# The S5 mixer's block kernel: two buffers, the diagonal on TensorE, and a new order of DMA issues on ScalarE

## The chip, the cores and the metric

The kernel runs on one core of one Trainium2 chip. The metric is the device time of one execution in microseconds; of several runs the median is taken. All data are fp32 (products use fp32 or its split in a high and a low part).

## What is computed

The program is two transformer-like blocks one behind the other. The change lies in the first, in one of its two mixers, the S5 mixer, which works on 64 groups of 16 channels with 64 complex states each:

```python
bu_re = jnp.einsum('blgh,gph->blgp', u, bb_re)
bu_im = jnp.einsum('blgh,gph->blgp', u, bb_im)
_, _, s_re, s_im = lax.associative_scan(combine, (a_re, a_im, bu_re, bu_im), axis=1)
y = (jnp.einsum('blgp,ghp->blgh', s_re, c_re.astype(f32))
     - jnp.einsum('blgp,ghp->blgh', s_im, c_im.astype(f32))
     + u * d_skip.astype(f32))
y = jax.nn.gelu(y.reshape(bsz, length, D_S5), approximate=False)
v = y @ w_glu.astype(f32) + b_glu.astype(f32)
y = v[..., :D_S5] * jax.nn.sigmoid(v[..., D_S5:])
```

The term `u * d_skip` is a diagonal matrix of 16 x 16 for each group. It can be added to the first tap (lag 0) of the kernel with which a group's inputs are convolved, and that is what is done here.

## The kernel before

The eight groups of a block are worked together, so there are eight blocks, i = 0 to 7 (NT = 8). Time is cut in pieces of LB = 8 steps. What lies within a piece is a product with a small lower-triangular block matrix (tile mt, made of the eight lags of the kernel ka); what crosses pieces goes through the states, with a scan over 65 pieces.

For block i these steps follow each other:

- VectorE, `s5_tables`: products of powers into ba and cab (L1342 to L1351). It waits for the k product of block i-1 and, ahead of writing cab (L1347), for the y product of block i-2.
- TensorE, `s5_bat_pe` (L1424): ba turned. ScalarE, `s5_bat_act` (L1508): the copy bat.
- TensorE, `s5_k_pe` (L1433): the eight lags of the kernel into PSUM. ScalarE, `s5_kernel_act` (L1516): the copy ka, in one buffer, for which it waits until the moves of block i-1 have landed (L1514); behind it the two copies to dec (L1519).
- VectorE, `s5_diagonal` (L1363, L1367): dd is d_skip on a diagonal; it is added to lag 0 of ka.
- ScalarE's DMA queue, `s5_move` (L1526): eight DMAs put ka, shifted by a lag each, into mt.
- TensorE, `s5_w_pe` (L1444), VectorE, `s5_scan` (L1379 to L1394), TensorE, `s5_y_pe` (L1457 from the states, L1465 from mt).
- ScalarE: Gelu into yk (L1559); its DMA queue, `s5_y_out` (L1538): eight DMAs write yk to memory, in another order of elements; GpSimd's queue, `s5_y_back` (L1330), reads it back as yf; ScalarE, `s5_hi` (L1530), and VectorE, `s5_lo` (L1399), split it into hhi and hlo for the gated unit.

The order on each engine is written out by hand. On VectorE (`s5_dve`) an iteration i is scan(i), diagonal(i+1), tables(i+2), lo(i-2). On ScalarE (`s5_act`) it is move(i+1), in some iterations the rows of the modulation (L762), Gelu(i), bat(i+2), y out(i), kernel copy(i+2), hi(i-1), in some iterations the columns of the modulation (L772). On TensorE (`s5_pe`) it is y(i), w(i+1), bat(i+2), k(i+2), in iterations 1, 3, 4, 6 and 7 the turn of the modulation (L780), and between all of them the products with the modulation's weights (L752), whose tile wada holds eight units and is loaded by SyncE's queue. These products belong to the second block of the network; they fill the time in which TensorE would wait. The gated unit (L338) follows the last iteration.

An engine that issues a DMA executes the issue in its own program order.

## Time and profile before

| | us |
|---|---|
| median of 3 runs | 2908.52 |
| lowest, highest run | 2907.16, 2919.92 |
| span of the profiled execution | 2895.8 |
| TensorE busy in it | 2800.7 |
| VectorE busy | 1503.3 |
| ScalarE busy | 1083.2 |
| GpSimd busy | 1268.2 |

The span goes from the first to the last instruction of the one profiled execution. The eight blocks lie between about 355 and 500 us of it. In the rows below, PE is TensorE, PEld its weight loads, DVE VectorE, ACT ScalarE, POOL GpSimd, SP SyncE; a name with q behind it (ACTq) is that engine's DMA issues. Times are in us unless ns is said; a row of the timeline is start, duration, engine, line, operation, output<-inputs, count, and in brackets the idle time ahead of it and what ended it. "Issue" stands where the profile shows nothing that was waited for. Issues of DMAs are not counted as busy.

### The profile page before, as it was taken

What the parts mean: (1) busy time and instruction counts of PE and PEld (TensorE: products, weight loads), DVE (VectorE), ACT (ScalarE), POOL (GpSimd) and SP (SyncE); (2) the same over time, 40 slices, a digit from 0 to 9 for tenths busy, and PEclk for the clock granted to TensorE, in tenths of its full rate; (3) what the DMA queues carried; (4) which work ended last, traced back from release to release, by engine and by line L of the source; (5) the groups of instructions that cost most, each with busy time, mean ns of one, the idle gap of its engine ahead of it and who ended that gap; (6) DMA issues with size and microseconds to landing.
All of it is one profiled execution on the core that took longest, in us unless ns stands there. A gap on an engine that the chain in (4) does not pass through costs nothing.

```text
span 2895.8 us, 41246 instructions
## 1 busy us (share of the span) xinstructions
PE 2800.7 (97%) x15682; PEld 2290.9 (79%) x15682; DVE 1503.3 (52%) x1968; ACT 1083.2 (37%) x1662; POOL 1268.2 (44%) x696
## 2 busy tenths in 40 slices
PE   7999988999999999999999999999999999999998
PEld 6985744878888888877787888888887778788887
DVE  6865585353332345358875532422454887452535
ACT  4435223333332323235543422322343554342433
POOL 3444201434354264278842323222347884344343
PEclk9999999999999999999999999999999999999999
DMA  5335498323232243432222212121233222233232
GB/s 174 99 102 203 148 312 239 123 86 104 80 110 86 90 129 118 157 104 90 70 87 66 73 52 72 65 66 59 62 106 111 94 66 88 80 102 95 94 102 73
DMA packets 116008, 306.89 MB, mean 106 GB/s; under 512 B 36176, under 2 KB 44496, under 8 KB 115344
## 3 DMA queue, kind: packets, MB, share of 16 engines
q1 hardware_dynamic: 87584, 284.49, 30.6%
q10 hardware_dynamic: 27712, 18.50, 2.3%
q8 instruction: 101, 1.65, 0.2%
q0 software_dynamic: 560, 1.84, 0.2%
q14 instruction: 51, 0.42, 0.0%
HBM read 294.95 MB, written 7.45 MB: 104 GB/s over the span
## 4 chain that ended last, share of the span: by engine, by line
PE 85%; DVE 4%; DMA 2%; issue 2%; POOL 2%; ACT 2%; DVEq 1%; ACTq 1%; SPq 0%; POOLq 0%
PE ps L304 41%; PE ps L338 17%; PE ps L329 6%; PE ps L1955 3%; PE ps L1951 3%; PE ps L1956 3%; PE ps L1959 3%; POOL wlo L265 2%; PE ps L2368 2%; PE ps L2028 1%; PE ps L2009 1%; DMA mt<-ka 1%; PE ps L752 1%; DVE nacc L451 1%; PE ps L1997 1%
## 5 line engine op out<-in xcount | busy, mean ns | idle before, releaser
L265 POOL TENSOR_TENSOR wlo<-wraw,whi 128x1024 fp32r<-128x1024 f32 x373 | 919.8, 2476 | 1316.1 <-ACT whi L257 1313.7
L257 ACT ACTIVATE whi<-wraw 128x1024 fp32r<-128x1024 f32 x373 | 392.1, 1055 | 458.0 <-PE ps L304 170.4
L304 PE MATMUL ps<-xah,whi 128*128 128x512 f32 x992 | 388.2, 391 | 1.7 <-issue 1.7
L304 PE MATMUL ps<-xal,whi 128*128 128x512 f32 x992 | 387.8, 391 | 0.0
L304 PE MATMUL ps<-xah,wlo 128*128 128x512 f32 x992 | 280.2, 391 | 0.0
L2254 DVE SCALAR_TENSOR_TENSOR co<-ub,vec,co 128x512 f32<-128x512 f32 (+1 forms) x216 | 255.7, 1222 | 4.2
L304 PEld LDWEIGHTS ps<-xah,whi 128*128 128x128 f32 x992 | 186.1, 188 | 42.7 <-issue 2.7
L304 PEld LDWEIGHTS ps<-xah,wlo 128*128 128x128 f32 x992 | 186.2, 188 | 40.0
L304 PEld LDWEIGHTS ps<-xal,whi 128*128 128x128 f32 x992 | 186.2, 188 | 40.1
L2355 POOL TENSOR_TENSOR co<-co,ct 128x512 f32<-128x512 f32 (+1 forms) x144 | 164.7, 1144 | 21.7 <-issue 1.8
L304 PE MATMUL ps<-hhi,whi 128*128 128x512 f32 x408 | 159.4, 391 | 0.0
L304 PE MATMUL ps<-hlo,whi 128*128 128x512 f32 x408 | 158.9, 389 | 0.0
L1113 DVE SCALAR_TENSOR_TENSOR res<-ps,mod,res 128x512 f32<-128x512 f32 (+1 forms) x64 | 47.6, 748 | 201.6 <-PE ps L329 110.0
L2711 DVE SCALAR_TENSOR_TENSOR f<-ps,vec,f 128x511 f32<-128x511 f32 x88 | 50.1, 611 | 196.7 <-ACT f L2672 196.7
L1955 PE MATMUL ps<-xah,whi 128*128 128x512 f32 x352 | 143.6, 408 | 4.2 <-DVE ub L2266 2.6
L2353 POOL TENSOR_TENSOR ct<-ub,vec 128x512 f32<-128x512 f32 (+1 forms) x144 | 136.7, 950 | 22.5 <-issue 12.4
L1956 PE MATMUL ps<-xal,whi 128*128 128x512 f32 x352 | 137.7, 391 | 0.0
L2669 ACT ACTIVATE f<-ps,vec 128x512 f32<-128x512 f32 x44 | 34.3, 778 | 187.0 <-PE ps L329 179.3
L1111 DVE TENSOR_TENSOR res<-res,ps 128x512 f32<-128x512 f32 x48 | 33.0, 687 | 132.1 <-PE ps L304 70.2
L304 PE MATMUL ps<-hhi,wlo 128*128 128x512 f32 x408 | 100.9, 389 | 0.0
L329 PE MATMUL ps<-xchi,whi 128*128 128x256 f32 x352 | 99.6, 283 | 0.0
L329 PE MATMUL ps<-xchi,wlo 128*128 128x256 f32 x352 | 99.4, 282 | 0.0
(415 smaller groups left out, 5978.5 us busy)
## 6 DMA issues: line engine op xcount, KB each, us to landing
wraw<-stream SPq DMA_DIRECT2D x425, 512.0 KB, 3.5
wada<-w_ada SPq DMA_DIRECT2D x56, 512.0 KB, 7.0
wraw<-w_ada SPq DMA_DIRECT2D x40, 512.0 KB, 3.8
biasb<-attn_bias ACTq DMA_DIRECT2D x32, 256.0 KB, 3.4
xin<-x0T SPq DMA_DIRECT2D x4, 528.0 KB, 6.2
s_u<-uk ACTq DMA_DIRECT2D x8, 264.0 KB, 2.7
res<-x0T ACTq DMA_DIRECT2D x1, 2048.0 KB, 9.3
outT<-res SPq DMA_DIRECT2D x4, 512.0 KB, 2.6
```

Source lines behind the costliest of these rows:

```text
L257: act.activation(whi[:, s], wraw[:, s], ACT.Copy).then_inc(hi_done[s], 1)
L265: pool.tensor_tensor(wlo[:, s], wraw[:, s], whi[:, s].bitcast(F32), ALU.subtract).then_inc(lo_done[s], 1)
L304: last = pe.matmul(ps[:, bank, 0:b - a], w[:, s, kt], x[:, kt, c0 + a:c0 + b], start=start, stop=stop)
L329: return pe.matmul(ps[:, R + s, 0:CTX], w[:, s, kt], part[:, kt], start=start, stop=stop)
L338: last = pe.matmul(ps[:, bank, 0:b - a], w[:, s, kt], x[:, kt, c0 + a:c0 + b], start=start, stop=stop)
L1951: last = pe.matmul(o, wraw[:, s, kt], x1[:, kt, 0:p.T], start=kt == 0, stop=kt == NT - 1)
L1955: pe.matmul(o, whi[:, s, kt], xah[:, kt, 0:p.T], start=kt == 0, stop=False)
L1956: pe.matmul(o, whi[:, s, kt], xal[:, kt, 0:p.T], start=False, stop=False)
L1959: last = pe.matmul(o, wlo[:, s, kt], xah[:, kt, 0:p.T], start=False, stop=kt == NT - 1)
L2254: dve.scalar_tensor_tensor(o, ub[:, m, k:k + p.T], colr(f"dw{p.l}", 1, k * 4 + m), o, ALU.mult, ALU.add)
L2353: pool.tensor_tensor(ct[:, 0:T], ub[:, m, k:k + T], colr(f"dw{l}", 1, k * 4 + m).to_broadcast([P, T]), ALU.mult)
L2355: ins = pool.tensor_tensor(o, o, ct[:, 0:T], ALU.add)
```

## The change

The tiles ka and dd get two buffers, ka1 in a place where the last parts of hlo will be, dd in another place. VectorE only makes dd, at the start of `s5_tables`; `s5_diagonal` is gone with its semaphore. `s5_k_pe` adds dd to lag 0 in PSUM by products with the identity. The two copies to dec move from behind ka to ahead of bat. On ScalarE the kernel copy(i+2) comes directly behind bat(i+2), the move(i+2) directly behind that, and y out(i) behind the moves; the copy into ka waits for the moves of block i-2.

```diff
--- before.py
+++ after.py
@@ -1166,8 +1166,8 @@
     u3a = at("u3a", [P, 2, 8, NB], Z2 + 11072)
     u3b = at("u3b", [P, 8, NB], Z2 + 30400)
     u3 = [u3a[:, 0], u3a[:, 1], u3b[:, :]]
-    ka = at("ka", [16, 8, LB, 16], Z2 + 15296)
-    dd = at("dd", [16, 8, 16], Z2 + 19392)
+    ka = [at("ka0", [16, 8, LB, 16], Z2 + 15296), at("ka1", [16, 8, LB, 16], O_HL + 12 * K)]
+    dd = at("dd", [16, 2, 8, 16], O_KC + 6208)
     d5 = at("d5", [16, S5_G], Z2 + 19904)
     yk = at("yk", [P, 2, 8, SEQ // 8], Z2 + 20160)
     yf = at("yf", [P, 2, SEQ], Z2 + 24256)
@@ -1192,8 +1192,7 @@
     s_yw = [sem(f"s5_y_written{b}") for b in range(2)]
     s_yr = [sem(f"s5_y_landed{i}") for i in range(NT)]
     e_pa, e_pv = steps("s5_param_scalar", "step", "mag", "sin"), steps("s5_param_vector", "ls", "angle", "kept")
-    f_tab, f_ka, f_v, f_l = (steps("s5_tables", "tab"), steps("s5_diagonal", "ka"), steps("s5_scan", "rot", "sp"),
-                             steps("s5_lo", "lo"))
+    f_tab, f_v, f_l = steps("s5_tables", "tab"), steps("s5_scan", "rot", "sp"), steps("s5_lo", "lo")
     f_hd, f_w, f_y = steps("s5_head", "bat", "k"), steps("s5_states", "w"), steps("s5_output", "y")
     f_a, f_g, f_h = steps("s5_head_copied", "bat", "kac"), steps("s5_gelu", "g"), steps("s5_hi", "hi")
     f_d = [sem(f"s5_kernel_moved{b}") for b in range(2)]
@@ -1333,6 +1332,8 @@
 
         pr = slice(4 * i, 4 * i + 4)
         dve.wait_ge(f_hd.sem, f_hd.past("k", i, 1))
+        dve.tensor_tensor(dd[:, i % 2], ident[0:16, 0:16].unsqueeze(1).to_broadcast([16, 8, 16]),
+                          d5[:, 8 * i:8 * i + 8].unsqueeze(2).to_broadcast([16, 8, 16]), ALU.mult)
         b = cab[:, i % 2]
 
         def product(o, n, x, w, neg):
@@ -1358,15 +1359,6 @@
         product(ba, 8, (s5bar[:, 0, pr], s5bar[:, 1, pr]), (s5pwr[:, 0, :, pr], s5pwr[:, 1, :, pr]), False)
         product(b, 9, (cc5[:, 0, pr], cc5[:, 1, pr]), (s5pw[:, 0, :, pr], s5pw[:, 1, :, pr]), True).then_inc(f_tab.sem, 1)
 
-    def s5_diagonal(dve, i):
-
-        dve.tensor_tensor(dd[:, :], ident[0:16, 0:16].unsqueeze(1).to_broadcast([16, 8, 16]),
-                          d5[:, 8 * i:8 * i + 8].unsqueeze(2).to_broadcast([16, 8, 16]), ALU.mult)
-        dve.drain()
-        dve.wait_ge(f_a.sem, f_a.past("kac", i))
-        dve.tensor_tensor(ka[:, :, 0], ka[:, :, 0], dd[:, :], ALU.add).then_inc(f_ka.sem, 1)
-        dve.drain()
-
     def s5_scan(dve, i):
         pr = slice(4 * i, 4 * i + 4)
         dve.wait_ge(f_w.sem, f_w.past("w", i))
@@ -1406,8 +1398,6 @@
     def s5_dve(dve):
         for i in range(NT):
             s5_scan(dve, i)
-            if i + 1 < NT:
-                s5_diagonal(dve, i + 1)
             if i + 2 < NT:
                 s5_tables(dve, i + 2)
             if i >= 2:
@@ -1426,12 +1416,19 @@
 
     def s5_k_pe(pe, i):
         pe.wait_ge(f_a.sem, f_a.past("kac", i, 1))
+
+        def lags(p, r):
+            for g in range(2):
+                h = slice(64 * g, 64 * g + 64)
+                last = pe.matmul(ps[0:16, head_bank(i) + 2 + g, p * P:(p + 1) * P], ba[h, r, p, LB - 1],
+                                 cab[h, i % 2, r, p, 0:8].rearrange("p k h -> p (k h)"), start=r == 0, stop=r == 1)
+            return last
+
         for p in range(4):
-            for r in range(2):
-                for g in range(2):
-                    h = slice(64 * g, 64 * g + 64)
-                    last = pe.matmul(ps[0:16, head_bank(i) + 2 + g, p * P:(p + 1) * P], ba[h, r, p, LB - 1],
-                                     cab[h, i % 2, r, p, 0:8].rearrange("p k h -> p (k h)"), start=r == 0, stop=r == 1)
+            lags(p, 0)
+            for g in range(2):
+                pe.matmul(ps[0:16, head_bank(i) + 2 + g, p * P:p * P + 16], ident[0:16, 0:16], dd[:, i % 2, 2 * p + g], start=False, stop=False)
+            last = lags(p, 1)
         last.then_inc(f_hd.sem, 1)
 
     def s5_w_pe(pe, i):
@@ -1505,25 +1502,25 @@
 
         b = head_bank(i)
         act.wait_ge(f_hd.sem, f_hd.past("bat", i))
+        for r in range(2):
+            act.activation(dec[:, i % 2, r, :, 1:], s5m8[:, 4 * i:4 * i + 4].unsqueeze(2).to_broadcast([P, 4, NBW - 1]), ACT.Copy)
         act.activation(bat[:, :], ps[:, b:b + 2].rearrange("p r (q m) -> p r q m", q=4), ACT.Copy).then_inc(f_a.sem, 1)
 
     def s5_kernel_act(act, i):
 
         b = head_bank(i)
         act.wait_ge(f_hd.sem, f_hd.past("k", i))
-        if i:
-            act.wait_ge(f_d[(i - 1) % 2], 128 * ((i - 1) // 2 + 1))
-        act.activation(ka[:, :].rearrange("p (q g) k h -> p g q (k h)", g=2),
-                       ps[0:16, b + 2:b + 4].rearrange("p g (q m) -> p g q m", q=4), ACT.Copy)
-        for r in range(2):
-            ins = act.activation(dec[:, i % 2, r, :, 1:], s5m8[:, 4 * i:4 * i + 4].unsqueeze(2).to_broadcast([P, 4, NBW - 1]), ACT.Copy)
-        ins.then_inc(f_a.sem, 1)
+        if i >= 2:
+            act.wait_ge(f_d[i % 2], 128 * (i // 2))
+        act.activation(ka[i % 2][:, :].rearrange("p (q g) k h -> p g q (k h)", g=2),
+                       ps[0:16, b + 2:b + 4].rearrange("p g (q m) -> p g q m", q=4), ACT.Copy).then_inc(f_a.sem, 1)
 
     def s5_move(act, i):
 
-        act.wait_ge(f_ka.sem, f_ka.past("ka", i))
+        act.wait_ge(f_a.sem, f_a.past("kac", i))
         for k in range(LB):
-            act.dma_start(mt[16 * k:16 * k + 16, i % 2, :, 16 * k:], ka[:, :, 0:LB - k].rearrange("p g k h -> p g (k h)")).then_inc(f_d[i % 2], 16)
+            act.dma_start(mt[16 * k:16 * k + 16, i % 2, :, 16 * k:],
+                          ka[i % 2][:, :, 0:LB - k].rearrange("p g k h -> p g (k h)")).then_inc(f_d[i % 2], 16)
 
     def s5_hi(act, i):
         act.wait_ge(s_yr[i], 16)
@@ -1539,14 +1536,11 @@
 
     def s5_act(act):
         act.wait_ge(s_m0, 1)
-        s5_bat_act(act, 0)
-        s5_kernel_act(act, 0)
-        s5_move(act, 0)
-        s5_bat_act(act, 1)
-        s5_kernel_act(act, 1)
+        for i in range(2):
+            s5_bat_act(act, i)
+            s5_kernel_act(act, i)
+            s5_move(act, i)
         for i in range(NT):
-            if i + 1 < NT:
-                s5_move(act, i + 1)
             if i in ADA_END:
                 ada_rows(act, ADA_END[i])
             if i == NT - 1:
@@ -1560,12 +1554,12 @@
                            ps[:, 6:8, 0:4 * (NBW - 1)].rearrange("p g (q c) -> p g q c", q=4), ACT.Gelu).then_inc(f_g.sem, 1)
             if i + 2 < NT:
                 s5_bat_act(act, i + 2)
+                s5_kernel_act(act, i + 2)
+                s5_move(act, i + 2)
             if i + 1 < NT:
                 s5_y_out(act, i)
             else:
                 split_hi(act, U_GLU + R - 1)
-            if i + 2 < NT:
-                s5_kernel_act(act, i + 2)
             if i:
                 s5_hi(act, i - 1)
             if i in ADA_END and i + 1 < NT:
@@ -2980,7 +2974,6 @@
             for m in range(R, NT - 1):
                 add_unit_dve(dve, U_OUT1 + m, 0, 0, m, res, SEQ, r=r)
             dve.drain()
-            s5_diagonal(dve, 0)
             s5_tables(dve, 1)
             add_unit_dve(dve, U_OUT1 + NT - 1, 0, 0, NT - 1, res, SEQ, r=r)
             dve.drain()
```

## Rows read from the trace of the kernel before

**Rows 1.** The page, the whole span: its first line, and the chain by engine.
```profile
span 2895.8 us, 41246 instructions
...
PE 85%; DVE 4%; DMA 2%; issue 2%; POOL 2%; ACT 2%; DVEq 1%; ACTq 1%; SPq 0%; POOLq 0%
```

**Rows 2.** Windows: length, PE, PEld, DVE, ACT, POOL busy (count), PEclk, DMA share, GB/s.
```profile
418.00:435.00 17.00, 12.81 (x204) 6.39 (x203) 14.61 (x25) 5.53 (x9) 0.54 (x1) 1.00 1.10 333
```

**Rows 3.** Waits from 368 to 500 us: total, times, longest.
```profile
ACT ka L1516 <- DMA mt<-ka: 16.1, 3, 7.9
PE ps L1424 <- DVE cab L1351: 14.5, 6, 4.2
...
DVE ka L1367 <- ACT dec L1519: 11.8, 6, 5.1
```

**Rows 4.** Timeline of VectorE, one block (iteration 3).
```profile
418.14 0.69 DVE L1379 TENSOR_TENSOR t<-ps,ej 128x520 f32<-128x520 f32 x1
...
423.90 0.28 DVE L1363 TENSOR_TENSOR dd<-cst,d 16x128 f32<-16x128 f32 x1
425.76 0.28 DVE L1367 TENSOR_TENSOR ka<-ka,dd 16x128 f32<-16x128 f32 x1 [1.57 <-ACT dec L1519]
...
434.43 0.69 DVE L1399 TENSOR_TENSOR hlo<-yf,hhi 128x512 fp32r<-128x512 f32 x1
435.04 0.69 DVE L1379 TENSOR_TENSOR t<-ps,ej 128x520 f32<-128x520 f32 x1
```

**Rows 5.** Timeline of VectorE and TensorE, the start of the stage.
```profile
360.33 0.28 DVE L1367 TENSOR_TENSOR ka<-ka,dd 16x128 f32<-16x128 f32 x1 [2.22 <-ACT dec L1519]
...
385.30 1.09 PE L1424 MATMUL ps<-cst,ba 128*128 128x128 f32 x8 [2.06 <-DVE cab L1351]
...
388.13 1.92 PE L1433 MATMUL ps<-cab,ba 64*16 64x128 f32 x32
```

**Rows 6.** Timeline of TensorE, the end of the stage.
```profile
487.08 1.84 PE L780 MATMUL ps<-cst,ar 128*128 128x6 f32 x8 [4.52 <-issue]
...
490.65 1.99 PE L1457 MATMUL ps<-spv,cab 64*64 64x64 f32 x64
...
498.20 0.94 PE L338 MATMUL ps<-hhi,whi 128*128 128x512 f32 x3
```

**Rows 7.** Timeline of ScalarE: one block from 418 to 433, and single rows around it.
```profile
400.27 0.60 ACT L1559 ACTIVATE yk<-ps 128x512 f32<-128x512 f32 x1
...
418.63 1.02 ACT L1508 ACTIVATE bat<-ps 128x1024 f32<-128x1024 f32 x1 [2.72 <-PE ps L1424]
418.69 4.01 ACTq L1538 DMA_DIRECT2D s_y<-yk  x8
424.10 1.01 ACT L1516 ACTIVATE ka<-ps 16x1024 f32<-16x1024 f32 x1 [4.45 <-DMA mt<-ka]
425.02 0.71 ACT L1519 ACTIVATE dec<-ks 128x256 f32<-128x256 f32 x2
425.63 0.61 ACT L1530 ACTIVATE hhi<-yf 128x512 fp32r<-128x512 f32 x1
426.07 5.71 ACTq L1526 DMA_DIRECT2D mt<-ka  x8
431.95 1.79 ACT L762 ACTIVATE ar<-ps 2x512 f32<-2x512 f32 x3 [5.71 <-issue]
...
468.68 5.17 ACTq L1538 DMA_DIRECT2D s_y<-yk  x8
477.59 1.01 ACT L1516 ACTIVATE ka<-ps 16x1024 f32<-16x1024 f32 x1 [7.95 <-DMA mt<-ka]
...
487.00 0.60 ACT L1559 ACTIVATE yk<-ps 128x512 f32<-128x512 f32 x1
```

**Rows 8.** Landing times by line: L1538 (y out), then L1330 (y back).
```profile
DMA to landing us min/median/max: 1.7/4.9/10.1
...
DMA to landing us min/median/max: 2.8/7.4/8.5
```

## Prediction

> **What bounds the kernel now.** First the page as a whole: the span is 2895.8 us and TensorE carries 85% of the chain that ended last [rows 1]. That average says nothing of the stage that the change touches, so next come the windows, by stage. In one block of the S5 mixer (there are eight, from 370 to 498 us) TensorE is busy 12.8 of 17 us, the DMA share is 1.10, and VectorE is busiest with 14.6 of 17 us [rows 2]. A few microseconds are open here. The waits of this stretch give the order of work: TensorE waits 14.5 us for VectorE's tables (L1351), VectorE waits 11.8 us ahead of the diagonal's add (L1367) for ScalarE, and ScalarE waits 16.1 us ahead of the copy of the kernel (L1516) until the moves of the block before have landed [rows 3]. It is a ring: copy into ka, add on VectorE, tables on VectorE behind the add, TensorE's products, the next copy; the single buffer ka keeps the ring closed until eight moves are down.
>
> Last, VectorE's own block in the timeline [rows 4]: scan at 418.14, dd at 423.90, the add at 425.76 after 1.57 us of waiting, hlo at 434.43, next scan at 435.04. The period is 16.9 us. Without the wait and without the add (0.28 us and about as much for its drain, some 0.5) it is 16.9 - 1.57 - 0.5 = **14.9 us**.
>
> **The change, part by part.**
>
> The start of the stage. VectorE's diagonal of block 0 ends with a wait of 2.22 us [rows 5] and stands ahead of the tables of block 1. These tables still wait for TensorE's k product of block 0, which the diagonal's products now lengthen. Of the 2.8 us (wait and add) I count 1.1 us as gained, since the k product ended about 1.7 us ahead of the add; the bounds are 0.3 and 2.0.
>
> The diagonal on TensorE: eight more products per block, 16 records if they split in two as the others do. The nearest row is the k product itself, 32 records in 1.92 us, 0.06 us each [rows 5]; the far side is the turn L780, 8 records of 128 rows and columns in 1.84 us, 0.23 us each [rows 6]. So 1.0 to 3.7 us per block; I take **1.0**, because the new products load 16 columns of weights as the k product does. It lies in TensorE's idle time, 17 - 12.8 = 4.2 us per block [rows 2]; if that cover were gone it would cost 1.0 us in each of eight blocks. dd (0.28 us) stays on VectorE and loses its drain. The two copies to dec (0.7 us) move ahead of bat on ScalarE, where only the turn (L780) waits for bat soon.
>
> The waits that go. ScalarE's 16.1 us and VectorE's 11.8 us [rows 3] disappear by construction: the other buffer has been free for a block, and nobody adds on VectorE any more. If VectorE alone set the pace, the gain would be 11.8, plus 0.5 for each of seven adds, plus 1.1: 16.4 us. That is the ceiling.
>
> What is late next is ScalarE. It issues its DMAs itself, and an issue holds it. One block in the new order, by [rows 7]: dec 0.71, bat 1.02, ka 1.01, eight moves 5.71, eight writes of y 4.01 to 5.17 (I take 4.4), hhi 0.61, yk 0.60, and about 0.5 for the hand-overs between them. That is **14.6 us**, and 1.8 more where L762 copies the rows of the modulation, which three of the five steps from yk of block 1 to yk of block 6 have. The mean is 15.7 us, above VectorE's 14.9. ScalarE becomes the pace.
>
> It pulls VectorE along. hhi (L1530) now comes behind eight moves and eight writes. In the old order it came 1.5 us after ka began, at 425.63 [rows 7], and hlo (L1399), which waits for it, at 434.43 [rows 4]: 8.8 us of cover. The new order puts about 10 us of issues ahead of hhi, so the cover is gone and hlo waits for hhi by 1 to 3 us a block. Queued behind hlo on VectorE is the next scan, and TensorE's y product waits for the scan. This is a new wait, and it stands where the old one stood.
>
> The sum on ScalarE. TensorE's bat product of block 2 started at 385.30 and its k product ended at 390.05, 4.75 us later [rows 5]. The tables ahead of it come 1.1 + 0.5 us earlier, at 383.7. So the k product ends at 383.7 + 4.75 + 1.0 = 389.5, ka at 390.5, the moves at 396.2, y of block 0 at 400.6, L762 at 402.4. There yk of block 1 starts, **2.1 us later** than before (400.27 [rows 7]). Five blocks of 14.6 and three times 1.8 are 78.4 us: yk of block 6 starts at 480.8, against 487.00 [rows 7]. The gain is made at the end, where the old order waited 7.95 us for a landing ahead of ka at 477.59 and then issued eight moves before L762. hhi of block 4 ends ahead of L762, at 479.0, hlo at 479.6, the last scan takes 5.8 (418.14 to 423.90 [rows 4]): the y product of block 7 starts at 485.6 instead of 490.65 [rows 6]. That is 5.0 us. What follows it (the products that keep TensorE warm, the turn, the gated unit at 498.20 [rows 6]) waits for nothing that is later than this, and moves along.
>
> The way of y. hhi of a block also needs y written to memory and read back: from the last write issued to its landing 4.9 (median) to 10.1 us, back 7.4 (median) to 8.5 us [rows 8], and 0.5 for the hand-over. This length L is 12.8 to 19.1 us, its middle 16.0. The new order leaves it one block of ScalarE, 15.7 us. What it is over costs ScalarE every second block, since the next write starts late as well: (16.0 - 15.7) / 2 x 5 blocks = 0.8 us. Before, y was issued some 10 us earlier in the block and this was hidden.
>
> **Sum: 5.0 - 0.8 = 4.2 us gained.** The sum is made on the traced execution, whose span is 2895.8 us; the median of the runs is 2908.5, and the 12.7 us between them stay. 2908.5 - 4.2 = **2904.3 us**.
>
> On the issues, rows and page differ. Sixteen issues hold ScalarE for 9.7 us, as long as such a transfer takes to land [rows 7, 8]. The Trainium skill, "DMA: Bandwidth & Descriptors", section "Issuing engines are not separate DMA queues", calls the sequencer's time to start a DMA "usually small relative to the DMA itself". By that rule the place of moves and y on ScalarE would be of no weight, and the time would be that of rival A at its ceiling.
>
> **Rivals.**
>
> A, VectorE sets the pace. If the moves issue in 5.2 and y in 3.9 us (5.71 and 4.4 taken above), ScalarE's block is 1.0 us shorter on six blocks: 4.2 + 6 = 10.2 us, 2898.3; the ceiling of 16.4 us gives 2892.1. For it: single blocks reach 4.01 [rows 7]. Against: the same traffic is to pass in less time, and the share of the DMA engines is at 1.10 already [rows 2].
>
> B, the DMA engines eat the gain. Moves and y are now issued back to back, and the block has the same bytes in a shorter time. If L is 17.8, (17.8 - 15.7) / 2 x 5 = 5.3 us go and nothing is gained: 2908.8. With 19.1, the largest sum of the rows, it is 2912.0. For it: 333 GB/s in a block whose share is full [rows 2]. [...] The Trainium skill's same page, "Where 436 GB/s comes from", puts the ceiling of the ports at 435 GB/s; by it the 333 x 17 = 5.7 MB of a block would take an estimated 13.0 us, and this rival would be out.
>
> C, slower. The mechanism of B one step on, at L1530: ScalarE stands there for y on its way back, and with it every later bat, ka, move and L762, and TensorE's turn behind L762. It decides from L = 17.8. At L = 22 (landings of 12 and 9.5, beyond any row at this load) (22 - 15.7) / 2 x 5 = 15.8 us go, and the time is 2908.5 + 10.8 = 2919.3.
>
> D, the change does not do what it says: TensorE's diagonals cost 3.7 us a block, near its 4.2 us of idle time, so ka starts later by the 2.7 us over my count and the second buffer saves little. 2907.0.
>
> **How the numbers follow.** Forecast, a gain of 2 to 8 us, 0.50; A 0.15; B 0.22; C 0.07; D 0.06. The likeliest gives 2904.3. The range of 8 in 10 takes in the larger part of A and B: 2895.5 to 2912.0. By 0.5% I mean 14.5 us, about what a measurement of this kernel can tell from no change. A gain of that size needs the ceiling of A: 0.04. A loss of that size needs C beyond L = 23: 0.04. The rest, 0.92, is no change.
>
> **What would show it.** Right: no wait of ScalarE ahead of ka for moves, no wait of VectorE behind dd; instead VectorE waits ahead of hlo for hhi in blocks 2 to 6; ScalarE has nearly no idle time from 390 to 480; yk starts in block 1 later than 400.27 and in block 6 at 479 to 483; the gated unit starts near 493. For A: hlo waits for nothing, and the gated unit starts before 489. For B and C: ScalarE waits at L1530 for yf by 2 us or more in several blocks, with landings of y past 10 us. For D: the k product longer than 4 us. The prediction is wrong in its frame if anything outside 355 to 515 us changes by more than a microsecond or two.

## The result and the profile after

The changed kernel takes 2912.98 us (median of 20 runs), the kernel before 2906.96 us in the runs beside it. The ratio is **1.0019, interval 1.001 to 1.0028**: 5.5 us slower (6.0 by the medians), where 4.2 us faster were forecast. All differences in this document are below half a percent. One of the 20 runs of the kernel before took 4673.15 us and is no part of the ratio.

First the page of the changed kernel, its span and its chain by engine. TensorE's share of the chain is 87%, where it was 85% [rows 1]. This says nothing of the stage.

```profile
span 2910.5 us, 41476 instructions
...
PE 87%; DVE 4%; issue 2%; ACT 2%; POOL 2%; ACTq 1%; DVEq 1%; DMA 1%; SPq 0%; POOLq 0%
```

The spans differ by 14.7 us, and the marks of the stage divide them. Its first product with w starts at 364.24 before and 369.88 after, its last yk at 498.47 and 515.24. So 5.6 us arise ahead of the stage, **11.1 us in it** (134.2 and 145.4 us), and behind it 2.1 us are gained back. Of the 11.1 us, 4.2 arise up to yk of block 1 (40.3 us after the first product with w, before 36.0), 4.4 from there to yk of block 6 (91.2 and 86.7 us), and 2.5 behind that. Next the waits of the changed kernel from 368 to 505 us (total, times, longest), to be held against [rows 3].

```profile
DVE hlo L1391 <- ACT hhi L1527: 25.6, 5, 14.2
ACT dec L1506 <- PE ps L1414: 16.5, 4, 10.1
...
ACT ka L1515 <- PE ps L1423: 15.6, 5, 4.8
...
PE ps L1414 <- ACT mod L772: 5.3, 1, 5.3
...
PE ps L780 <- ACT bat L1507: 3.8, 2, 2.1
...
PE ps L1414 <- DVE cab L1352: 3.5, 3, 2.3
```

ScalarE's wait for the moves and VectorE's wait ahead of the add are gone. TensorE's wait for the tables fell from 14.5 to 3.5 us. In their place VectorE waits 25.6 us for hhi, ScalarE waits for TensorE's products in four or five blocks, and TensorE waits for ScalarE: for the bat copy, and in one block for the columns of the modulation (L772).

ScalarE's timeline over two blocks (start, duration; brackets: idle time before, and its releaser). ACTq rows are issues.

```profile
444.85 0.60 ACT L1553 ACTIVATE yk<-ps 128x512 f32<-128x512 f32 x1
445.35 0.71 ACT L1506 ACTIVATE dec<-ks 128x256 f32<-128x256 f32 x2
445.96 1.01 ACT L1507 ACTIVATE bat<-ps 128x1024 f32<-128x1024 f32 x1
446.86 1.00 ACT L1515 ACTIVATE ka<-ps 16x1024 f32<-16x1024 f32 x1
447.89 5.94 ACTq L1522 DMA_DIRECT2D mt<-ka  x8
453.92 4.29 ACTq L1535 DMA_DIRECT2D s_y<-yk  x8
458.25 0.63 ACT L1527 ACTIVATE hhi<-yf 128x512 fp32r<-128x512 f32 x1 [10.40 <-issue]
...
458.99 1.79 ACT L762 ACTIVATE ar<-ps 2x512 f32<-2x512 f32 x3
460.80 0.60 ACT L1553 ACTIVATE yk<-ps 128x512 f32<-128x512 f32 x1
...
461.90 1.01 ACT L1507 ACTIVATE bat<-ps 128x1024 f32<-128x1024 f32 x1
465.07 1.01 ACT L1515 ACTIVATE ka<-ps 16x1024 f32<-16x1024 f32 x1 [2.15 <-PE ps L1423]
466.11 5.85 ACTq L1522 DMA_DIRECT2D mt<-ka  x8
472.05 6.28 ACTq L1535 DMA_DIRECT2D s_y<-yk  x8
478.38 0.63 ACT L1527 ACTIVATE hhi<-yf 128x512 fp32r<-128x512 f32 x1 [12.31 <-issue]
478.92 0.17 ACT L772 ACTIVATE mod<-ps 128x24 f32<-128x24 f32 x1
478.99 0.59 ACT L1553 ACTIVATE yk<-ps 128x512 f32<-128x512 f32 x1
```

In the first block ScalarE is late: ka follows bat at once, since the k product had ended at 445.0 us, ahead of the bat copy. This block is the forecast's 14.6 + 1.8 us, and it took 15.95. In the second block ScalarE is early for ka and **stands still between bat and ka**, because TensorE has not made the k product yet. (Between the bat product and the k product TensorE also runs eight products of the modulation, L752, 1.88 us in the rows below. They are part of this gap, and no run here moves them.) There the old order issued y: 4.01 us of issues in an idle time of 4.45 us [rows 7]. (In that row the moves of the block before ended the wait, in others the k product; the second buffer takes away the former and leaves the latter.) The new order does nothing in this gap and adds y's 4 to 6 us behind the moves. The block takes 18.2 us.

The other side of this ring on TensorE, from 459 to 490 us, and on VectorE at its end:

```profile
459.11 1.06 PE L1414 MATMUL ps<-cst,ba 128*128 128x128 f32 x8
460.10 1.88 PE L752 MATMUL ps<-wada,cs 128*2 128x512 f32 x8
461.91 0.40 PE L1423 MATMUL ps<-cab,ba 64*16 64x128 f32 x4
462.23 0.26 PE L1430 MATMUL ps<-dd,cst 16*16 16x16 f32 x4
...
479.24 1.94 PE L1414 MATMUL ps<-cst,ba 128*128 128x128 f32 x8 [5.28 <-ACT mod L772]
481.11 3.44 PE L752 MATMUL ps<-wada,cs 128*2 128x512 f32 x8
...
487.52 1.89 PE L752 MATMUL ps<-wada,cs 128*2 128x512 f32 x12
```

```profile
499.51 0.69 DVE L1391 TENSOR_TENSOR hlo<-yf,hhi 128x512 fp32r<-128x512 f32 x1 [14.18 <-ACT hhi L1527]
```

The columns L772 stand behind moves, y and hhi, so they come at 478.92 (above). TensorE's bat product of block 7 waits for them, 5.28 us, and starts at 479.24. Its k product ends at 487.5, ka follows at 487.64, eight moves at 488.68, eight writes of y at 494.62, hhi at 498.85. VectorE has stood 14.18 us for that hhi with the last scan queued behind it. After its idle time TensorE ran slower (last section): the bat product took 1.94 instead of 1.06 us and the eight L752 products 3.44 instead of 1.88. So of ScalarE's waits in this block some 0.9 of the 1.63 us ahead of dec and 1.6 of the 4.79 us ahead of ka belong to the clock.

### The profile page after: what moved, and what is told of

It is laid out like the page before. It is cut to its first block, busy times and chain, and to the rows that moved or that the text cites. A ratio compares the mean times of both kernels' runs of the same rounds, so it can differ in the third digit from the quotient of the medians.

```text
span 2910.5 us, 41476 instructions
## 1 busy us (share of the span) xinstructions
PE 2820.1 (97%) x15810; PEld 2299.2 (79%) x15810; DVE 1501.7 (52%) x1960; ACT 1083.1 (37%) x1662; POOL 1272.5 (44%) x696
## 3 DMA queue, kind: packets, MB, share of 16 engines
q0 software_dynamic: 560, 1.84, 0.2%
## 4 chain that ended last, share of the span: by engine, by line
PE 87%; DVE 4%; issue 2%; ACT 2%; POOL 2%; ACTq 1%; DVEq 1%; DMA 1%; SPq 0%; POOLq 0%
PE ps L304 41%; PE ps L338 17%; PE ps L329 6%; PE ps L1949 3%; PE ps L1945 3%; PE ps L1950 3%; PE ps L1953 2%; PE ps L2362 2%; POOL wlo L265 2%; PE ps L752 2%; PE ps L2022 1%; PE ps L2003 1%; ACTq L1522 1%; DVE nacc L451 1%; ACTq L1535 1%
## 5 line engine op out<-in xcount | busy, mean ns | idle before, releaser
L304 PEld LDWEIGHTS ps<-xal,whi 128*128 128x128 f32 x992 | 186.1, 188 | 40.3
L2347 POOL TENSOR_TENSOR ct<-ub,vec 128x512 f32<-128x512 f32 (+1 forms) x144 | 136.9, 951 | 22.5 <-issue 12.3
```

Source lines behind the costliest of these rows:

```text
L304: last = pe.matmul(ps[:, bank, 0:b - a], w[:, s, kt], x[:, kt, c0 + a:c0 + b], start=start, stop=stop)
L2347: pool.tensor_tensor(ct[:, 0:T], ub[:, m, k:k + T], colr(f"dw{l}", 1, k * 4 + m).to_broadcast([P, T]), ALU.mult)
```

## The experiments

Each kernel was run 5 to 12 times (the changed one 20 times) beside the kernel before. The last columns are the start of the first product with w and of the last yk in the profiled execution, and the length between them, in us.

| kernel | against | time / before, us | ratio (95%) | first w, last yk | length |
|---|---|---|---|---|---|
| before | | | | 364.24, 498.47 | 134.2 |
| changed | | 2912.98 / 2906.96 | 1.0019 (1.001 to 1.0028) | 369.88, 515.24 | 145.4 |
| after_again | changed, identical | 2911.55 / 2906.49 | 1.0017 (1.0004 to 1.003) | 370.49, 516.64 | 146.2 |
| f1_old_order | changed, old order | 2894.37 / 2904.06 | 0.9964 (0.9951 to 0.9977) | 364.53, 494.01 | 129.5 |
| f7_hhi_behind | f1, hhi last | 2896.0 / 2906.49 | 0.9955 (0.9939 to 0.9971) | 372.00, 501.15 | 129.2 |
| f10_cols_last | f1, L772 last | 2897.44 / 2906.52 | 0.9971 (0.996 to 0.9981) | 366.90, 496.56 | 129.7 |
| f3_cols_first | changed, L772 ahead of moves | 2903.43 / 2904.06 | 1.0003 (0.999 to 1.0016) | 364.49, 501.95 | 137.5 |
| f9_y_before_moves | f3, y ahead of moves | 2904.08 / 2906.52 | 0.9997 (0.9985 to 1.0009) | 368.04, 504.89 | 136.9 |
| f4_y_gpsimd | changed, y on GpSimd | 2899.4 / 2904.06 | 0.9979 (0.9968 to 0.999) | 371.20, 501.59 | 130.4 |
| f5_old_order_y_gpsimd | f1, y on GpSimd | 2896.0 / 2906.52 | 0.9963 (0.9951 to 0.9976) | 368.30, 500.51 | 132.2 |
| b1_y_behind_ka | before, y behind ka | 2912.25 / 2906.52 | 1.0016 (1.0003 to 1.0028) | 365.87, 508.15 | 142.3 |
| c3_te_diag | before, diagonal on TensorE | 2898.1 / 2904.06 | 0.9988 (0.9974 to 1.0002) | 363.81, 497.07 | 133.3 |
| d4_two_buffers | before, two buffers | 2901.42 / 2906.49 | 0.9977 (0.9965 to 0.9988) | 365.91, 496.92 | 131.0 |
| f6_old_order_late_glu | f1, later weight loads | 2899.49 / 2906.49 | 0.997 (0.9955 to 0.9984) | 364.29, 491.93 | 127.6 |

**The theory**: the two buffers and the diagonal on TensorE help, the order of issues on ScalarE costs more than they bring, and it costs because y's issues left the gap between bat and ka. **The rivals**: a part other than the order costs; it is the landing of y, or its place behind the moves; hhi's place costs; the columns' place costs.

### f1_old_order: the parts in the old order

```
             if i + 2 < NT:
                 s5_bat_act(act, i + 2)
-                s5_kernel_act(act, i + 2)
-                s5_move(act, i + 2)
             if i + 1 < NT:
                 s5_y_out(act, i)
...
+            if i + 2 < NT:
+                s5_kernel_act(act, i + 2)
             if i:
                 s5_hi(act, i - 1)
             if i in ADA_END and i + 1 < NT:
                 ada_cols(act, ADA_END[i])
+            if i + 2 < NT:
+                s5_move(act, i + 2)
```

> The changed kernel with only ScalarE's order undone: y out ahead of the copy of ka, hhi and the columns ahead of the moves. Two buffers, the diagonal on TensorE and dec's place stay. Theory O (the order costs the time: hhi and the columns of the modulation stand behind 10 us of issues): the waits ahead of hlo vanish, TensorE no longer waits for the columns (5.28 us) ahead of the bat product of block 7, and the time is 3 to 8 us below the kernel before (ratio 0.9972 to 0.9990), since the waits for landed moves and for the add are gone too. Theory T (TensorE's longer product, 3.0 instead of 1.9 us a block, costs the time): the ratio stays at 1.001 to 1.003, as for the changed kernel.

Measured: 0.9964, somewhat below the range expected under theory O. Theory T falls: TensorE's product is the longer one here too. Against the changed kernel the stage is 15.9 us shorter, and 0.0055 of 2907 us are 16.0. ScalarE's timeline, one block:

```profile
444.85 0.60 ACT L1553 ACTIVATE yk<-ps 128x512 f32<-128x512 f32 x1
...
445.95 1.01 ACT L1507 ACTIVATE bat<-ps 128x1024 f32<-128x1024 f32 x1
446.34 2.94 ACTq L1535 DMA_DIRECT2D s_y<-yk  x6
449.89 1.01 ACT L1515 ACTIVATE ka<-ps 16x1024 f32<-16x1024 f32 x1 [2.93 <-PE ps L1423]
451.59 0.63 ACT L1527 ACTIVATE hhi<-yf 128x512 fp32r<-128x512 f32 x1 [0.68 <-DMA yf<-s_y]
...
452.22 5.32 ACTq L1522 DMA_DIRECT2D mt<-ka  x7
457.64 0.60 ACT L1553 ACTIVATE yk<-ps 128x512 f32<-128x512 f32 x1 [5.35 <-issue]
```

y is issued between bat and ka, inside the wait for the k product, and the block takes 12.8 us (the one before it, with L762, 15.05). The order alone turns a loss into a gain, so no other part is the cause of the loss. Of theory O's signs one came only in part: hlo waits for nothing in the first four blocks, but 4.06 us ahead of the last scan.

y is free only as far as it fits into the gap. Ahead of the last ka, that of block 7, the issues take longer (six of the eight are shown), and ka waits for them and not for the k product:

```profile
460.95 6.54 ACTq L1535 DMA_DIRECT2D s_y<-yk  x6
467.59 1.01 ACT L1515 ACTIVATE ka<-ps 16x1024 f32<-16x1024 f32 x1 [5.89 <-issue]
```

### after_again: the changed kernel once more

> The changed kernel unchanged, on the same chip and against the same runs as the three others, with a second trace. If the loss belongs to the stage: ratio 1.001 to 1.003, and the stage from the first w product to the last yk again 8 us or more longer than the 134.2 us of before, with TensorE waiting for the columns ahead of the bat product of block 7 and the last scan behind hhi again. If the 5.6 us that the stage began later in the first trace (369.9 against 364.2) belong to the change, the first w product is again near 370; if they are chance, near 365.

Measured: 1.0017, a stage of 146.2 us, and the same pattern: VectorE waits 25.8 us in 5 for hhi (longest 13.9), ScalarE 15.8 us in 5 for the k product, TensorE 6.5 us in 3 for L772. The loss and its rows are no accident of one execution. The first product with w came at 370.49 us, again late, which the expectation had taken as a sign that the change causes it. But f1, f3 and f6 contain the same parts and have it at 364.3 to 364.5, so this sign decides nothing (last section).

### c3_te_diag and d4_two_buffers: one part alone

c3 keeps one ka and its old order, and puts the diagonal on TensorE (with the two copies to dec ahead of bat, as in the change):

```
+            for g in range(2):
+                pe.matmul(ps[0:16, head_bank(i) + 2 + g, p * P:p * P + 16], ident[0:16, 0:16], dd[:, i % 2, 2 * p + g], start=False, stop=False)
...
-            if i + 1 < NT:
-                s5_diagonal(dve, i + 1)
```

> The kernel before with the diagonal on TensorE alone (and dec ahead of bat): one buffer ka, the old order on ScalarE. Theory O: VectorE's 11.8 us of waits ahead of the add go, but the copy of ka still waits for the landed moves: 0 to 4 us below before, ratio 0.9985 to 1.000. Theory T: 1 to 5 us above before, ratio 1.0005 to 1.002.

d4 keeps the diagonal on VectorE and gives ka two buffers:

```
-        if i:
-            act.wait_ge(f_d[(i - 1) % 2], 128 * ((i - 1) // 2 + 1))
-        act.activation(ka[:, :].rearrange("p (q g) k h -> p g q (k h)", g=2),
+        if i >= 2:
+            act.wait_ge(f_d[i % 2], 128 * (i // 2))
+        act.activation(ka[i % 2][:, :].rearrange("p (q g) k h -> p g q (k h)", g=2),
```

> The kernel before with two buffers for ka alone; the diagonal stays on VectorE, the order is the old one. With c3_te_diag (0.9988, the diagonal alone) and f1_old_order (0.9964, both) this makes a square. If the two parts add up: 0.9976, 7 us below before. If one needs the other (the add on VectorE still waits for ka, and the tables for the add): 0.9985 to 1.000. VectorE's 11.8 us of waits ahead of the add fall to 4 to 8.

Measured: 0.9988, whose interval holds 1, and 0.9977. Their product is 0.9965, and f1 with both has 0.9964: within the intervals they add up. The first row below is of c3, from its waits; the other two of d4.

```profile
ACT ka L1515 <- DMA mt<-ka: 35.0, 5, 10.8
```

```profile
PE ps L1424 <- DVE cab L1351: 13.3, 6, 3.1
...
DVE ka L1367 <- ACT dec L1519: 8.9, 6, 3.4
```

With one buffer, taking the add off the path sends the time to the wait for the moves: 35.0 us in 5, where it was 16.1 in 3 [rows 3]. Both sums hold y's issues, which the view counts as idle. From the end of the last of them to ka it is 16.9 us in c3 and 5.8 in before. With two buffers that wait is gone, and the wait ahead of the add stays with 8.9 of 11.8 us, somewhat more than the 4 to 8 expected. Each part opens only its own half of the ring.

### f3_cols_first: the columns ahead of the moves

```
                 s5_kernel_act(act, i + 2)
+            if i in ADA_END and i + 1 < NT:
+                ada_cols(act, ADA_END[i])
+            if i + 2 < NT:
                 s5_move(act, i + 2)
...
             if i:
                 s5_hi(act, i - 1)
-            if i in ADA_END and i + 1 < NT:
-                ada_cols(act, ADA_END[i])
```

> The changed kernel with the columns of the modulation (L772) moved ahead of the moves, directly behind the copy of ka; y and hhi stay behind the moves. Theory O1 (the wait of the bat product of block 7 for the columns, 5.28 us, and the waits of ka, 4.79, and of hlo, 14.18, that follow are the loss): 6 to 10 us below the changed kernel, ratio to before 0.998 to 1.000. Theory O2 (hhi behind moves and y is the loss in every block): less than 3 us of difference to the changed kernel, ratio 1.001 to 1.002.

Measured: 1.0003. From the changed kernel's 1.0019 that is 0.0016 or 4.7 us, with intervals that overlap, between what the two theories expected; the stage is 7.9 us shorter. TensorE no longer waits for L772. The view of waits puts 33.8 us in 3 ahead of hhi down to yf, but nearly all of it is issues. The longest real wait is here:

```profile
412.25 5.26 ACTq L1535 DMA_DIRECT2D s_y<-yk  x8
418.83 0.63 ACT L1527 ACTIVATE hhi<-yf 128x512 fp32r<-128x512 f32 x1 [11.70 <-DMA yf<-s_y]
```

From the last issue of y to hhi it is 1.32 us, and 0.05 and 0.04 us in the two others: 1.4 us for the way of y in all. The larger part of the 16 us to f1 is still missing, and this left the places of y and hhi.

### f7_hhi_behind: only hhi behind the moves

```
-            if i:
-                s5_hi(act, i - 1)
             if i in ADA_END and i + 1 < NT:
                 ada_cols(act, ADA_END[i])
             if i + 2 < NT:
                 s5_move(act, i + 2)
+            if i:
+                s5_hi(act, i - 1)
```

(against f1)

> The changed kernel with y out and the columns back in their old places, and only hhi left behind the moves. Between f1_old_order (0.9964: all three ahead) and f3_cols_first (1.0003: y and hhi behind). If hhi behind 6 us of moves is what costs, through hlo and the next scan: ratio 0.999 to 1.001. If y behind the moves costs (ScalarE waits for yf, landings late): ratio 0.996 to 0.998, as f1_old_order.

Measured: 0.9955, as fast as f1 within the intervals. hhi behind five to eight microseconds of moves costs nothing that these runs can tell; this rival falls.

### f9_y_before_moves: y out of the gap, yet ahead of the moves

```
                 s5_kernel_act(act, i + 2)
             if i in ADA_END and i + 1 < NT:
                 ada_cols(act, ADA_END[i])
-            if i + 2 < NT:
-                s5_move(act, i + 2)
             if i + 1 < NT:
                 s5_y_out(act, i)
...
+            if i + 2 < NT:
+                s5_move(act, i + 2)
             if i:
                 s5_hi(act, i - 1)
```

(against f3)

> The change with its two buffers and its diagonal on TensorE, but ScalarE's order in each iteration is: bat copy, ka copy, wada's columns, y out, moves, hhi. So y's issues are out of the gap between the bat copy and the ka copy, yet not behind the moves. Gap theory (y's issues of some 4 us were free because they lay in ScalarE's wait for the k product, and cost their length wherever else they stand): the ratio is like that of the kernel with the columns ahead of the moves and y behind them, 1.0003, so 0.998 to 1.002, with ScalarE's ka copy waiting 2 to 5 us for the k product in several blocks. Rival, behind-the-moves theory (it is y's late landing, a read that follows the moves' writes, that holds hhi and hlo): y lands early here, and the ratio is that of the kernel with y ahead of ka, 0.9955 to 0.997.

Measured: 0.9997, as f3, and outside the interval of f1 and of f7. One block of it on ScalarE:

```profile
440.93 1.01 ACT L1507 ACTIVATE bat<-ps 128x1024 f32<-128x1024 f32 x1
443.06 1.01 ACT L1515 ACTIVATE ka<-ps 16x1024 f32<-16x1024 f32 x1 [1.11 <-PE ps L1423]
444.04 0.19 ACT L772 ACTIVATE mod<-ps 128x24 f32<-128x24 f32 x1
444.10 5.26 ACTq L1535 DMA_DIRECT2D s_y<-yk  x8
449.39 5.40 ACTq L1522 DMA_DIRECT2D mt<-ka  x8
...
455.49 1.79 ACT L762 ACTIVATE ar<-ps 2x512 f32<-2x512 f32 x3
457.31 0.60 ACT L1553 ACTIVATE yk<-ps 128x512 f32<-128x512 f32 x1
```

y starts as ka ends and ScalarE waits for no yf, but the block is 17.5 us: 5.26 and 5.40 us of issues now both lie behind ka. The landing of y and its place behind the moves are out. What costs is that y's issues lie outside the gap.

### f4_y_gpsimd and f5_old_order_y_gpsimd: y's issues off ScalarE

Both take y_out of blocks 0 to 6 from ScalarE's list and put it ahead of y back on GpSimd; f4 keeps the changed order, f5 is f1 otherwise. (The last y has a semaphore of its own, since it stays on ScalarE.)

```
-            if i + 1 < NT:
-                s5_y_out(act, i)
-            else:
+            if i + 1 == NT:
                 split_hi(act, U_GLU + R - 1)
...
             for i in range(NT - 1):
+                s5_y_out(pool, i)
                 s5_y_back(pool, i)
```

> The changed kernel with y written by GpSimd's queue instead of ScalarE's, for blocks 0 to 6. ScalarE's block loses 4.4 us of issues; moves, hhi and columns keep their order. Theory O: ScalarE stops setting the pace, hlo waits for hhi by less than 2 us a block, VectorE sets the pace with 14.9 us a block: 10 to 18 us below the changed kernel, ratio to before 0.995 to 0.998. Rival G (GpSimd's queue needs more than the 4.4 us for eight writes and y comes back late): ScalarE waits ahead of hhi for yf instead and the ratio stays at 1.000 to 1.003. Theory T: ratio above 1.000.

> The kernel with y ahead of ka, hhi and the columns ahead of the moves, but its eight y issues are taken off ScalarE and given to GpSimd's queue for blocks 0 to 6. Gap theory: these issues cost ScalarE nothing between the bat copy and the ka copy, since it only waits there for the k product, so taking them away brings nothing: 0.9955 to 0.9975, as 0.9964 with them in place, and the ka copy's wait for the k product grows by about the 4 us that the issues took. Rival, load theory (ScalarE's whole sum of busy time and issues is the pace, so y's 4 us count anywhere): seven blocks by 4 us less, up to 28 us or 0.99, until VectorE's 15.0 us a block holds again, so 0.992 to 0.994.

Measured: 0.9979 and 0.9963. In the changed order, taking these issues away is worth 0.0040 or 11.6 us, in the old order nothing (0.9964 with them). f5's timeline, one block of ScalarE:

```profile
447.32 0.60 ACT L1553 ACTIVATE yk<-ps 128x512 f32<-128x512 f32 x1
...
449.41 1.00 ACT L1507 ACTIVATE bat<-ps 128x1024 f32<-128x1024 f32 x1
453.64 1.01 ACT L1515 ACTIVATE ka<-ps 16x1024 f32<-16x1024 f32 x1 [3.23 <-PE ps L1423]
```

From bat to ka it is 4.23 us with nothing issued in between, and 3.94 us in f1 with y's eight issues there. Over the six blocks 2 to 7 it is 27.3 us in f5 and 28.6 in f1, and the difference lies in f1's last block, where y's issues did not fit. **The gap is nearly as long without y in it as with it.** Of f5's expectation one part failed: the wait ahead of ka was to grow by about the 4 us of issues, and in the view it went from 24.0 us in f1 (18.1 for the k product and 5.9 as issue) to 22.7. The view counts issues as idle time, so it never showed y as filling the gap; only the distance from bat to ka does. f4 fell into its expected range; hlo waits in it for hhi in one block, 8.1 us ahead of the last scan.

### b1_y_behind_ka: the kernel before with y moved alone

```
             if i + 2 < NT:
                 s5_bat_act(act, i + 2)
+                s5_kernel_act(act, i + 2)
             if i + 1 < NT:
                 s5_y_out(act, i)
...
-            if i + 2 < NT:
-                s5_kernel_act(act, i + 2)
```

> The kernel before with one buffer and the diagonal on VectorE, where nothing is changed but the place of y out: behind the ka copy and dec, ahead of hhi. Gap theory: the order alone, without the buffers and the TensorE diagonal, costs what it cost in the changed kernel, since ScalarE waits for the k product or for the buffer with y's 4 us still to come: 1.001 to 1.005, the time per block longer by 1 to 3 us where ScalarE is late. Rival (the order costs only together with the moves put early, which fill the queue and ScalarE before y): no change, 0.999 to 1.001.

Measured: 1.0016, a stage of 142.3 us. One buffer, the diagonal on VectorE, every other place as it was: the move of y behind ka makes the kernel before slower by 4.7 us by itself. Here the moves are still issued an iteration later, behind hhi and y. So the loss doesn't need moves ahead of y: the other explanation written down for this run falls. With y gone from the gap the wait for the moves is a real one, 19.8 us in 3 with nothing issued in it, where before had 5.8.

### f10_cols_last: the columns' place alone

```
-            if i in ADA_END and i + 1 < NT:
-                ada_cols(act, ADA_END[i])
             if i + 2 < NT:
                 s5_move(act, i + 2)
+            if i in ADA_END and i + 1 < NT:
+                ada_cols(act, ADA_END[i])
```

(against f1)

> The change with y out ahead of the ka copy and hhi ahead of the moves, and only wada's columns left behind the moves. It tells the price of the columns' place alone. Ring theory (the bat product of block 7 waits on TensorE for the columns of iteration 4, which stand behind 6 us of moves): from 0.9964 it loses as much as the changed order lost against the one with the columns ahead, 0.0015 or some 4 to 5 us: 0.997 to 0.9985. Rival (the columns' place costs only because y's issues stand ahead of them as well, and has 4 us to spare without them): 0.9955 to 0.9968.

Measured: 0.9971, 2 us above f1 with overlapping intervals. The value lies at the edge of the first range, and its interval reaches into both. The trace is against the first theory's mechanism: TensorE does not wait for L772 at all, and the stage is 129.7 us against 129.5. The columns cost at most a little where y is in the gap, and 4.7 us by the ratios where it is not (f3 against the changed kernel). How much of the latter is real isn't settled more closely.

### f6_old_order_late_glu: the gated unit's first weights later

In f1, TensorE still waits 4.6 us in 3 for wada (longest 4.0). f6 issues the four loads of the gated unit's weights one block later:

```
-                if i == NT - 3:
+                if i == NT - 2:
                     segment(U_GLU, U_GLU, R)
```

> f1_old_order with the four weight loads of the gated unit issued by SyncE behind the last of the modulation's loads instead of ahead of the last eight. In f1_old_order TensorE waits 4.6 us for wada in block 6, and writes of y and moves take 6.5 and 8.1 us to issue there. If the transfers bound that block: these waits fall under 1 us and the time is 3 to 7 us below f1_old_order, ratio to before 0.994 to 0.9955. If the loads then come late for whi (ScalarE's splits from 487 us on), TensorE waits for wlo instead and the ratio stays at 0.996 to 0.997.

Measured: 0.997, no gain over f1's 0.9964, though the stage of the profiled execution is the shortest, 127.6 us. The wait for wada fell to 1.4 us, but eight moves still took 8.11 us to issue in that block, and the gated unit then waits 3.1 us for wlo, as the second expectation had it.

The fastest kernels are thus f1 and f7, the two parts of the change with y ahead of ka, 0.9964 and 0.9955, and f5 with y on GpSimd, 0.9963. All three are faster than both kernels of the case.

## Why the prediction was wrong, point by point

**The frame.** "Nothing changes by more than a microsecond or two outside" did not hold in the trace: 5.6 us arose ahead of the changed code (last section). The ratio is little touched by it, since it comes from many runs.

**The median and the trace.** The sum was carried from the traced execution to the median with its 12.7 us kept. Of the 13 other profiled kernels the median lies 0.6 below to 9.0 us above the span, on average 4.2 above. The traced execution of before was a short one. In all 13 comparisons its stage of 134.2 us makes the others look 2 to 9 us slower than the ratios do (f1: 4.7 us gained in the stage, 10.5 by the ratio). That its own stage was short by some 4 to 5 us follows from this but wasn't seen in a second trace of it. Against such a base even a right sum would be too pessimistic, so this isn't the error.

**What bounds.** The ring was read rightly, its two waits went as told, and ScalarE did become what is late. But one of the waits was read too large. The 16.1 us for the moves [rows 3] hold y's issues; from the last issue to ka it was 1.40, 0.67 and 3.74 us, 5.8 in all. The 7.95 us ahead of ka at 477.59, on which the gain at the end was built, held 5.17 us of issues [rows 7].

**Small slips.** 16.9 - 1.57 - 0.5 is 14.8, not 14.9. hhi's end at 479.0, hlo and 5.8 us of scan make 485.5, not 485.6. A write of y lands after 4.9 us in the median and only the latest after 10.1 [rows 8], so 9.7 us of issues are longer than most landings. None of this moves the forecast.

**The start.** The bat product of block 2 started 18.7 us after the stage's first product, before 21.1: 2.3 us earlier, 1.6 were forecast. From it to the ka copy it took 7.6 us, not 4.75 + 1.0 + a hand-over. TensorE's clock was granted at 0.59 from 388 to 392 us, after an idle time of 2.25 us (before: 1.00 from 385 to 388, after 2.06 us), and L1414 took 1.92 instead of 1.09 us; the eight L752 products behind it took 2.69 instead of 1.88. yk of block 1 came at 410.15 - 5.64 = 404.5, 2.1 us behind the forecast 402.4.

**The diagonal on TensorE** was right: 16 records, 4 x 0.26 = 1.04 us a block. The k product as a whole takes 3.1 us instead of 1.92, short of the 4 us of rival D, which is out.

**The step that failed: ScalarE's block.** From yk of block 1 to yk of block 6 the sum said five times 14.6 and three times 1.8, 78.4 us. It took 501.32 - 410.15 = 91.2. By terms: the moves 28.55 us, forecast 5 x 5.71 = 28.55; y 24.9, forecast 22.0; L762 5.4 as forecast; copies 19.8 as forecast, the 2.5 us for hand-overs not needed; and **12.6 us of waits for TensorE, forecast nothing**: 0.81, 3.23, 2.15, 1.63 and 4.79 us ahead of dec and ka. The sum treated ScalarE's block as work laid end to end. But in it lies a dependence through TensorE: bat product, k product, ka, some 4.2 us from bat to ka when ScalarE is on time (f5). Of the 12.6 us, 10.2 lie ahead of ka, in this loop, and 2.4 ahead of dec. The old order had y in it, and [rows 7] showed that very thing: bat 418.63, y's issues 4.01 us beside it, ka 424.10. I put y's issues down as 4.4 us to be moved and not as 4.4 us that had been free.

**Rows and page on issues.** The page cited in the prediction, the Trainium skill, "DMA: Bandwidth & Descriptors", section "Issuing engines are not separate DMA queues", calls the time to start a DMA usually small relative to the DMA itself. For a single DMA the changed kernel's trace agrees: an issue of y took 0.47 us in the median, its landing 5.4. It does not follow that the place of eight issues has no weight. Here y's issues were worth 11.6 us behind ka (changed kernel against f4) and nothing ahead of it (f1 against f5). So my flat price per issue doesn't hold either; the price hangs on what the issuing engine waits for at that place.

**hlo's wait for hhi** was foreseen as 1 to 3 us a block. It was 25.6 us in 5: four of them make 11.4 us, the fifth 14.18. f7 shows that hhi's place did not make it: with hhi behind the moves hlo waits in none of the first four blocks. (Ahead of the last scan it waits 12.28 us there and 4.06 in f1, and the stage is as long in both.) hhi was late with ScalarE as a whole.

**The end.** hhi of block 4 was forecast to end at 479.0 and ended at 499.48 - 5.64 = 493.8, late by what the start and the blocks had lost. In it is a wait that I had not listed at all: L772 of iteration 4, ahead of the bat product of block 7 on TensorE. I had followed hhi and L762 behind the issues, but not L772. "Moves along" was not right either: from yk of block 6 to the last yk it took 13.9 us instead of 11.5, and what made this longer stays open.

**The way of y**: 0.8 us forecast. Writes landed after 1.7/5.4/11.5 us (minimum, median, maximum), reads back after 2.8/3.7/4.8, where the latter were 7.4 in the median [rows 8]. The length L is 5.4 + 3.7 + 0.5 = 9.6 us, not 16.0, and ScalarE waited for no yf in the changed kernel's profile (0.3 us once in after_again, where the view shows 10.4 us with the issues in it). **Rivals B and C** were the wrong mechanisms; f9, with y early, is as slow as f3. C had the sign right for a wrong reason. **Rival A** fails on the same waits. The rival that was missing is "ScalarE waits in the gap that y had filled".

## What to carry to other kernels

DMA issues that stand in an engine's wait for another engine are free as far as they fit into it. Count them at their full length as soon as an edit moves them out of it, and find such gaps by the distance between the two instructions around them, since a view of idle time doesn't show issues as work. When one engine's block is summed as the new pace, follow each of its inputs back through the other engines once, and add the part of that loop that nothing covers. When a change bundles buffers, a placement and an order, time the order alone: here two parts gained 0.36% together and the third gave more than that back.

## What the runs showed of the hardware that was not expected

TensorE's granted clock can differ for the same work, and fall after a short idle time. With no idle time before it, L1414 took 1.06 us at 459.11 in the changed kernel; after 5.28 us of idle it took 1.94 us at 479.24, and the clock from 476 to 482 us was 0.62 (1.00 is 2.4 GHz, half is the lower level). After 2.24 to 2.26 us of idle at the start of the stage it took 1.09 us (f3, f4), 1.18 (f9), 1.38 (after_again), 1.84 (f1) and 1.93 (f5): the same product, the same idle time.

Ahead of the stage, where the change touches nothing, the stretch from 325 to 335 us had this in before, then in the changed kernel (length, PE busy and count, PEld, DVE, ACT, POOL, PEclk, DMA share, GB/s):

```profile
325.00:335.00 10.00, 10.00 (x48) 8.36 (x47) 0.84 (x2) 0.09 (x1) 0.00 (x0) 0.96 0.27 47
```

```profile
325.00:335.00 10.00, 10.00 (x37) 8.29 (x37) 0.18 (x1) 0.27 (x1) 0.00 (x0) 0.72 0.31 51
```

TensorE is busy throughout in both, 48 against 37 records, at 0.96 and 0.72 of the clock. The stage's first product came at 363.8 to 365.9 us in seven of the profiled kernels, at 366.9 to 372.0 in the other seven. f7 with 372.00 is among the fastest and f3 with 364.49 isn't, so this decides no comparison here; what sets it stays open.
